# The first microseconds of a two-layer hybrid decoder step: where the norm gains load, when weight slots 1 to 3 are asked for, how the first squares are added, and how many matmuls run on ones

## What is computed

```python
def rmsnorm(x, gain):
    y = x * rsqrt(mean(x * x, axis=-1) + RMS_EPS)
    return y * gain
def hybrid_layer(x, ...):
    x = x + 0.5 * swiglu(rmsnorm(x, ffn1_norm), ffn1_w_gate, ffn1_w_up, ffn1_w_down)
    z = rmsnorm(x, mix_norm) @ w_in
    ...                       # attention, pooling, convolution and gating groups
    x = x + concat(groups) @ w_out
    x = x + 0.5 * swiglu(rmsnorm(x, ffn2_norm), ffn2_w_gate, ffn2_w_up, ffn2_w_down)
```

## Time and profile before

| | us |
|---|---|
| median of 3 runs | 1177.45 (1176.55 to 1178.22) |
| the profiled execution | 1176.97 |
| its span, first to last instruction | 1175.2 |
| TensorE busy | 1156.7 |
| VectorE busy | 763.9 |
| ScalarE busy | 530.7 |
| GpSimd busy | 118.5 |
| DMA | 180.24 MB, mean 153 GB/s |

### The profile page before, as it was taken

How to read it: one execution, slowest core, us unless ns; L and a number is a source line. 1 busy time by engine, 2 the same in 40 slices (tenths; PEclk the granted TensorE clock), 3 DMA queues, 4 the chain that set the end, 5 groups by cost and what they waited for, 6 DMA issues and landing times.

```text
span 1175.2 us, 22459 instructions
## 1 busy us (share of the span) xinstructions
PE 1156.7 (98%) x7942; PEld 1138.4 (97%) x7942; DVE 763.9 (65%) x1251; ACT 530.7 (45%) x787; POOL 118.5 (10%) x164
## 2 busy tenths in 40 slices
PE   8999999999899999999999999999989999999999
PEld 7999999998789999999999999999977999999998
DVE  7767665579957666655566667655898676666442
ACT  6444444444655444444444444444447454443332
POOL 0000000036900000000000000000676000000000
PEclk9999999999999999999999999999999999999999
DMA  7644435557326444435564444455672454444453
GB/s 239 209 151 150 146 105 155 153 179 228 128 89 187 157 144 151 144 110 149 168 208 149 153 144 142 117 148 170 187 239 73 129 169 153 143 155 126 137 147 105
DMA packets 71789, 180.24 MB, mean 153 GB/s; under 512 B 10122, under 2 KB 25282, under 8 KB 71746
## 3 DMA queue, kind: packets, MB, share of 16 engines
q1 hardware_dynamic: 71026, 178.36, 49.3%
q10 hardware_dynamic: 720, 1.34, 0.3%
HBM read 176.09 MB, written 3.58 MB: 153 GB/s over the span
## 4 chain that ended last, share of the span: by engine, by line
PE 89%; DVE 9%; DMA 1%; ACT 1%; issue 0%; ACTq 0%; DVEq 0%
PE bank L559 28%; PE bank L560 28%; PE bank L562 28%; DVE bank L1218 4%; DVE conv_y L1241 1%; DMA x<-in_xT 0%; DMA raw<-in_w 0%; PE bank L808 0%; ACT w_hi L880 0%; DVE tmp L1322 0%; PE bank L784 0%; PE bank L574 0%; DVE qk L1328 0%; DVE prob L1345 0%; PE bank L742 0%
## 5 line engine op out<-in xcount | busy, mean ns | idle before, releaser
L880 ACT ACTIVATE w_hi<-raw 128x1024 fp32r<-128x1024 f32 (+2 forms) x351 | 337.2, 961 | 476.9 <-PE bank L562 455.1
L559 PE MATMUL bank<-xg_hi,w_hi 128*128 128x320 f32 x1632 | 507.6, 311 | 1.3 <-DVE w_lo L1085 1.3
L562 PE MATMUL bank<-xg_hi,w_lo 128*128 128x320 f32 x1632 | 504.3, 309 | 0.0
L560 PE MATMUL bank<-xg_lo,w_hi 128*128 128x320 f32 x1632 | 504.3, 309 | 0.0
L1085 DVE TENSOR_TENSOR w_lo<-raw,w_hi 128x1024 fp32r<-128x1024 f32 (+2 forms) x319 | 347.7, 1090 | 154.0 <-ACT w_hi L880 149.4
L559 PEld LDWEIGHTS bank<-xg_hi,w_hi 128*128 128x128 f32 x1632 | 306.4, 188 | 5.0 <-issue 3.8
L560 PEld LDWEIGHTS bank<-xg_lo,w_hi 128*128 128x128 f32 x1632 | 306.4, 188 | 0.9
L562 PEld LDWEIGHTS bank<-xg_hi,w_lo 128*128 128x128 f32 x1632 | 306.4, 188 | 0.0
L559 PE MATMUL bank<-h_hi,w_hi 128*128 128x320 f32 x704 | 217.5, 309 | 0.0
L560 PE MATMUL bank<-h_lo,w_hi 128*128 128x320 f32 x704 | 217.5, 309 | 0.0
L562 PE MATMUL bank<-h_hi,w_lo 128*128 128x320 f32 x704 | 217.5, 309 | 0.0
(11 more groups left out here) (197 smaller groups left out, 751.7 us busy)
## 6 DMA issues: line engine op xcount, KB each, us to landing
raw<-in_w SPq DMA_DIRECT2D x223, 512.0 KB, 3.8
raw<-in_w SPq DMA_DIRECT2D x64, 384.0 KB, 3.1
raw<-in_w SPq DMA_DIRECT2D x64, 320.0 KB, 2.9
k_all<-in_cache_kT SPq DMA_DIRECT2D x32, 128.0 KB, 2.9
v_past<-in_cache_v SPq DMA_DIRECT2D x32, 128.0 KB, 3.1
x<-in_xT ACTq DMA_DIRECT2D x4, 320.0 KB, 5.6
out_yT<-x SPq DMA_DIRECT2D x1, 960.0 KB, 5.0
out_kT<-qk SPq DMA_DIRECT2D x2, 320.0 KB, 4.6
```

Source lines behind the costliest of these rows:

```text
L559: pe.matmul(out, hi, in_hi[:, k, :], start=first and m == 0, stop=False)
L560: pe.matmul(out, hi, in_lo[:, k, :], start=False, stop=False)
L562: mm = pe.matmul(out, lo, in_hi[:, k, :], start=False, stop=last and end)
L880: act.activation(w_hi[:, j, 0:count * P], raw[:, j, 0:count * P], ACT.Copy).then_inc(split_hi.sem, 1)
```

## The change

Four things, all in the first microseconds:

- `gain` is no longer the first load that ScalarE issues. SyncE issues it, between the two halves of slot 0.
- SyncE waits for the first quarter of x, not the second, before it asks for slots 1 to 3.
- The squares are added by tensor_tensor of two tiles at a time: tiles 0, 1 plus tiles 2, 3; tiles 4, 5 plus 6, 7; then the two results. The last one waits for the other two. TensorE's sum reads the two tiles that are left, `tmp[:, 0]` and `tmp[:, 1]`, instead of `sumsq` and `square[:, 0]`.
- 24 matmuls run on ones instead of 10.

```diff
-WARM_UPS = 10
+WARM_UPS = 24
...
             for n, signal in enumerate((raw_first_in, raw_in[0])):
                 cols = slice(n * 4 * P, (n + 1) * 4 * P)
                 sp.dma_start(raw[:, 0, cols], w8[W8_G1, 0, :, cols]).then_inc(signal.sem, 16)
-            sp.wait_ge(x_in[1].sem, 16)
+                if n == 0:
+                    sp.dma_start(gain[:, :], gains).then_inc(gain_in.sem, 16)
+            sp.wait_ge(x_in[0].sem, 16)
...
-                parts = (sumsq[:, :], square[:, 0, :]) if L == 0 and n == 0 else (sumsq[:, :],)
+                parts = (tmp[:, 0, :], tmp[:, 1, :]) if L == 0 and n == 0 else (sumsq[:, :],)
...
-            act.dma_start(gain[:, :], gains).then_inc(gain_in.sem, 16)
...
-            def sum_half(n, out, parts):
-
-                dve.wait_ge(squared_first.sem, (n + 1) * DT // 2)
-                dve.tensor_reduce(out, tmp[:, n * DT // 2:(n + 1) * DT // 2, :].rearrange("p d t -> p t d"), AX.X, ALU.add).then_inc(summed.sem, parts)
+            def sum_half(n):
+
+                first = n * DT // 2
+                dve.wait_ge(squared_first.sem, first + DT // 2)
+                dve.tensor_tensor(tmp[:, first:first + 2, :], tmp[:, first:first + 2, :], tmp[:, first + 2:first + 4, :],
+                                  ALU.add).then_inc(summed.sem, 1)
+
+            def sum_rest():
+
+                dve.wait_ge(summed.sem, 2)
+                dve.tensor_tensor(tmp[:, 0:2, :], tmp[:, 0:2, :], tmp[:, DT // 2:DT // 2 + 2, :], ALU.add).then_inc(summed.sem, DT - 1)
...
             split_low(0, BASE_G1, 0, 1, HALVES8)
-            sum_half(0, sumsq[:, :], DT // 2)
+            sum_half(0)
             split_low(0, BASE_G1, 0, 2, HALVES8)
-            sum_half(1, square[:, 0, :], DT // 2 + 1)
+            sum_half(1)
+            sum_rest()
             split_low(0, BASE_G1, 0, 3, HALVES8)
```

## The result

The changed kernel took 1179.34 us in the median of 22 runs (1176.15 to 1183.81), the kernel before 1176.95 us in 22 runs beside them. The ratio is 1.0020 with a 95% interval of 1.0011 to 1.0029: 2.4 us slower, where 1.2 us faster were forecast. The profiled execution took 1179.49 us, with a span of 1177.7 against 1175.2.

The account below looks back on a forecast made before the run. TensorE, busy 1156.7 of 1175.2 us, bounds the kernel; the gain is how much earlier the squares' sum begins. Column 1's 0.85 plus 0.34 us of waiting gives 1.19, so a median of 1176.25 us, range 1174.7 to 1178.1.

Parts of the forecast that it names:

- Slot 1's transfer: Load of slot 1 at the start: asked for at 6.05 instead of 7.22, landing at 10.96, between 10.56 and 11.56.
- The hole in 8:9: Stretch 8:9 us, where DMA engines moved only 147 GB/s against 412 in 6:7; the early request was to fill it.
- slot 1 comes no earlier: Rival: x's tail and slots 2 and 3 stretch slot 1's transfer; only 0.34 us remains, 1177.1 us; chance 0.25.
- Gains off ScalarE's queue: Start of x's load: issued 0.44 us earlier, of which 0.3 arrives; first quarter at 6.05 instead of 6.35.
- The gains themselves: Gains' load behind slot 0's first half: landing at 4.9, or 6.1 at worst; wanted at 6.05; cost at most 0.05.
- The ones: Matmuls ahead of column 0: end at 8.1 instead of 5.10, keep the clock up; worth 0.55 us on the path.
- That rival: The ones run at the low clock and delay column 0; costs from a rise at 5.7; 1179.1 or 1182.1 us; chance 0.08.
- The squares: Pair additions on VectorE, 0.82 us each, replace two 2.5 us reductions; 0.34 us of waiting before TensorE's squares' sum goes.
- I let the whole of it through to the end: Behind the loop's start at 26.59 TensorE waits only for engines; waits move along, so all 1.19 us reaches the end.
- The mechanism of the forecast: Start of the kernel: column 1 at 12.05 instead of 12.90, squares' sum at 19.2, loop's first matmul at 25.4.

Follow-up runs that it names:

- the wait alone: The kernel before, with only SyncE's wait ahead of slots 1 to 3 moved from x's second quarter to its first; ratio 1.0012, median 1178.06 us.
- The gains alone: The kernel before, with only the gains' load moved to SyncE, between slot 0's halves; ratio 1.0008.
- both remedies: Changed kernel, slots 1, 2, 3 asked for at x's first, third, last quarter, GpSimd's window sums behind eight biased scores; 0.9982, 1175.19 us (ones in a loop: 0.9986, 1175.75).
- requests one by one: The changed kernel, with slot 1 asked for at x's first quarter, slot 2 at its third and slot 3 at its last; ratio 1.0004.
- holding GpSimd back: The changed kernel, with GpSimd starting its window sums only after VectorE wrote the eight biased prompt scores; ratio 1.0002 (same wait in the kernel before: 0.9995).

## Why the prediction was wrong

- **Slot 1's transfer was the step that failed first.** I took 4.5 us plus 0.4, with an upper bound of 5.5. It was 7.3, and 6.6 with the wait alone changed. With it the loop began at 27.43 where the forecast had 25.4: 2.0 of the 3.6 us between forecast and measurement. The bound came from one x quarter's slowdown, for one transfer in x's tail. But three slots were asked for within 1.3 us, and they were served side by side (from x's last landing at 9.0 to slot 1's at 13.1 the engines moved 1.2 MB, over twice slot 1's): in the changed kernel slots 1, 2 and 3 landed 7.3, 8.2 and 8.9 us after their requests, before 4.5, 6.3 and 7.0. "The hole in 8:9" was no reserve. With the burst in it, the rate of 8:12 was 262 GB/s, only a little over before's 230. The rival "slot 1 comes no earlier" named the burst, but stopped at no gain; it lands later than before.
- **Gains off ScalarE's queue** brought x's first quarter at 5.7, 0.65 us earlier, over the upper bound of 0.44. The price lay where I charged nothing: slot 0's first half landed at 5.24 instead of 4.36, its second at 7.7 instead of my 6.5, and x's last quarter at 9.0 instead of 8.5. The gains themselves landed after 4.7 us, at 5.92, inside the bounds and 0.03 us ahead of their use. The gains alone put the loop at 27.70, 1.1 us late, through slot 1. The page on descriptors of the Trainium skill ("DMA: Bandwidth & Descriptors", Specifications) says that pieces under 512 B miss line rate; 28 KB took longer here than the 256 KB before it (4.7 against 4.5 us), so the trace agrees in direction, and their own landing cost nothing.
- **The ones** ended at 9.13, not 8.1: the clock rose at 6.1, not 4.2. It rose between 4.2 and 7.4 in the 17 profiled executions where it rose during the ones; in three with ten ones it hadn't risen when they ended, at 5.7 or 5.8. The Trainium skill's rule ("TensorE: Matmul & The Clock Gate", Part 1, What's actually happening) that the point varies from run to run holds here. My bound for this, a rise at 5.7, was right on cost (column 0 would have let column 1 start at about 12.5 instead of 12.05), but slot 1 covered it. That rival decided nothing in the changed kernel; with the burst gone the ones set column 0, and the loop began at 25.31 or 25.82 as they ended at 8.82 or 9.33. The clock didn't fall in column 0, as forecast.
- **The squares** were right: 0.83 us each, the 0.34 us of waiting gone, the low half of slot 3 not wanted sooner.
- **"I let the whole of it through to the end"** failed as well. From the loop's start to the first prompt score it held: 264.6 us before and after. But the attention stages hang on how GpSimd and VectorE fall together and on whether the clock falls ahead of the batch scores, and 56 instructions more on TensorE's queue shifted the first of these. In the profiled execution the stages took 1.7 us more, all of it in layer 1. Of this no rival told. In the row of waits it could be seen that the batch scores waited for VectorE twice, by unequal amounts (0.8 and 2.3 us): a stage whose length isn't fixed.
- The mechanism of the forecast was sound once the burst was gone: 12.18, 19.22 and 25.31 against 12.05, 19.2 and 25.4. And with both remedies in, the time fell by 1.8 us where 1.2 were forecast, but that nearness is in part luck: only 0.77 us of it is the start, and the rest comes from GpSimd's wait, which wasn't part of the change.

Open: what the 2.4 us of the median are made of beyond the start. The start was 0.84 and 1.00 us late in the two profiled executions of the changed kernel. Against the ratios of the changed kernel (1.0020 and 1.0015), requests one by one took about 1.9 us off, holding GpSimd back 1.5, and both together 4.5 or 3.9: each counts, and with intervals of 1 us to either side the sum is no contradiction. But the 1.5 us aren't the price of layer 0's late batch scores, which left the stage's length as it was in both traces; they hold a gain in layer 1 that has nothing to do with the change, and whatever falls of the clock go with the waits. Those falls weren't counted execution by execution. Why an instruction load lengthens SyncE's issue was not tested beyond that they coincide.

## What to carry to other kernels

An earlier request isn't an earlier landing. Before moving a group of transfers forward, count what is still under way at the new time, and ask first for the one that is wanted first, alone. When a change lengthens one engine's program, compare stages far behind it: wait lengths that differ between two passes through the same code mark a stage that a small shift can tip. What comes late costs only what isn't made up behind it: measure on to the next point at which the two kernels agree. And where GpSimd has work that isn't urgent, see what VectorE does beside it.

## What was not expected of the hardware

- Three 512 KB transfers asked for 1.3 us apart in all share the DMA engines from the start: the first took 4.5 to 7.5 us, growing with what else was under way, and 4.6 to 5.2 when asked for alone.
- SyncE's issue of a transfer took 1.35 us instead of 0.42 when it coincided with a 16 KB load of instructions on DMA queue 8; with the wait alone, where the load came 0.4 us behind the issue's start, it took 0.42.
- Eight taps of 128x64 on VectorE took 1.65 us in one execution with GpSimd idle beside them, 2.3 to 3.2 with its low halves beside a part of them, about 3.65 with low halves beside all, and 4.3 to 5.2 with its window sums beside them.
